# Two FFN weight sums change places in the upward pairs by seven products

## The reference, cut to what matters

```
def conv_ffn(h, w_up, conv_w, w_down):
    gu = causal_dwconv(h @ w_up, conv_w)        # h: 512 x 1024, w_up: 1024 x 5632
    g, u = jnp.split(gu, 2, axis=-1)
    return (jax.nn.silu(g) * u) @ w_down        # w_down: 2816 x 1024
...
x = x + conv_ffn(rmsnorm(x, norm_ffn_gain[i]), ffn_w_up[i], ffn_conv_w[i], ffn_w_down[i])
```

## Time and profile before

| | |
|---|---|
| time, median of 3 runs | 1220.42 us (1220.27 to 1220.99) |
| the profiled execution: time | 1220.91 us |
| the profiled execution: span | 1219.1 us |
| mean granted PE clock | 0.999 of full |
| PE busy | 1201.6 us (99%) |
| DVE, ACT, POOL busy | 757.1, 630.4, 740.3 us |
| first product of the first upward pair, end of the last | 856.37 us, 966.13 us |

### The profile page before, as it was taken

The page is one execution under the profiler, slowest core; times in us unless marked ns, Lnnn a source line. Parts: engine busy times, 40 slices in busy tenths (PEclk is TensorE's granted clock), DMA queues, the critical chain, the costliest instruction groups (busy, mean ns, idle before and its releaser), DMA issues.

```text
span 1219.1 us, 18895 instructions
## 1 busy us (share of the span) xinstructions
PE 1201.6 (99%) x6847; PEld 993.6 (82%) x6847; DVE 757.1 (62%) x1305; ACT 630.4 (52%) x1220; POOL 740.3 (61%) x561
## 2 busy tenths in 40 slices
PE   8999999999999999999999999999999999999997
PEld 6987777777888899987887777878888888889886
DVE  6555426757646777745697555447888865966234
ACT  6365535676644344455644666546545454333544
POOL 8674232353269776855384566548878775886842
PEclk9999999999999999999999999999999999999999
DMA  7322222122223333354142223323323343333332
GB/s 238 104 89 84 66 61 61 52 69 71 70 64 102 95 98 94 106 180 117 52 115 60 56 65 93 98 69 95 96 78 109 92 122 86 96 96 117 109 87 70
DMA packets 62437, 112.27 MB, mean 92 GB/s; under 512 B 6856, under 2 KB 11464, under 8 KB 62344
## 3 DMA queue, kind: packets, MB, share of 16 engines
q1 hardware_dynamic: 62200, 111.06, 31.6%
q10 hardware_dynamic: 144, 0.00, 0.0%
HBM read 108.87 MB, written 2.16 MB: 91 GB/s over the span
## 4 chain that ended last, share of the span: by engine, by line
PE 89%; DVE 6%; ACT 1%; issue 1%; POOL 1%; DMA 0%; SPq 0%; DVEq 0%; ACTq 0%; POOLq 0%
PE pb L1143 21%; PE pb L1144 20%; PE pb L1146 20%; PE pb L1205 4%; PE pb L1207 4%; PE pb L1206 4%; PE pb L1361 2%; DVE cv L2059 2%; PE pb L1337 2%; PE pb L1214 2%; PE pb L1304 1%; PE pb L1275 1%; PE pb L1277 1%; PE pb L1276 1%; PE pb L1258 1%
## 5 line engine op out<-in xcount | busy, mean ns | idle before, releaser
L2793 POOL TENSOR_TENSOR wlo<-raw,whi 128x512 fp32r<-128x512 f32 (+3 forms) x379 | 522.5, 1397 | 323.1 <-ACT whi L1554 322.1
L1143 PE MATMUL pb<-HH,whi 128*128 128x512 f32 x776 | 313.9, 405 | 0.0
L1144 PE MATMUL pb<-HL,whi 128*128 128x512 f32 x776 | 306.8, 395 | 0.0
L1146 PE MATMUL pb<-HH,wlo 128*128 128x512 f32 x776 | 306.1, 394 | 0.0
L1554 ACT ACTIVATE whi<-raw 128x512 fp32r<-128x512 f32 (+3 forms) x379 | 224.4, 614 | 107.7 <-PE pb L1146 55.5
L1143 PEld LDWEIGHTS pb<-HH,whi 128*128 128x128 f32 x776 | 146.2, 188 | 38.2 <-issue 4.6
L1144 PEld LDWEIGHTS pb<-HL,whi 128*128 128x128 f32 x776 | 146.0, 188 | 34.4 <-issue 2.9
L1146 PEld LDWEIGHTS pb<-HH,wlo 128*128 128x128 f32 x776 | 145.9, 188 | 34.5 <-POOL wlo L2793 0.4
L1690 ACT ACTIVATE P<-P,stat 128x256 f32<-128x256 f32 (+3 forms) x96 | 50.5, 527 | 78.5 <-DVE stat L2352 56.0
L2059 DVE SCALAR_TENSOR_TENSOR cv<-pb,vecs,cv 128x511 f32<-128x511 f32 x88 | 65.5, 745 | 4.8 <-ACT cv L1954 3.2
L2047 DVE TENSOR_TENSOR pb<-pb,rff 128x512 f32<-128x512 f32 x44 | 30.1, 694 | 38.5 <-PE pb L1146 31.7
(11 more groups left out here) (480 smaller groups left out, 2791.4 us busy)
## 6 DMA issues: line engine op xcount, KB each, us to landing
raw<-in_wall SPq DMA_DIRECT2D x368, 256.0 KB, 2.7
raw<-in_wall SPq DMA_DIRECT2D x8, 260.0 KB, 2.9
X<-in_xT SPq DMA_DIRECT2D x8, 256.0 KB, 5.6
X<-in_xT SPq DMA_DIRECT2D x2, 1024.0 KB, 7.3
outT<-PP SPq DMA_DIRECT2D x8, 256.0 KB, 2.5
raw<-in_wall SPq DMA_DIRECT2D x10, 192.0 KB, 2.4
raw<-in_wall SPq DMA_DIRECT2D x9, 128.0 KB, 2.3
cst<-in_cst SPq DMA_DIRECT2D x1, 832.0 KB, 7.8
```

Source lines behind the costliest of these rows:

```text
L1143: pe.do.matmul(b, hi, xh[k], start=start, stop=False, skip_group_check=tile[0] == "down")
L1144: pe.do.matmul(b, hi, xl[k], start=False, stop=False, skip_group_check=tile[0] == "down")
L1146: m = pe.do.matmul(b, lo, xh[k], start=False, stop=stop, skip_group_check=tile[0] == "down")
L2793: g.do.tensor_tensor(lo, x, hi.bitcast(F32), ALU.subtract).then_inc(*up(name, point))
```

## The change

In the upward pairs alone the unit and product order becomes A11, A22, S1, S2, S3, A12, S4: unit u+2 is now S1's, u+3 S2's. All of S1, S2 and S3 are summed by DVE, one behind the other, in split u+2. Nothing is computed otherwise. In `pair`, the steps that hang on product S2 keep their place behind it; as S1 is now no exception to the `split_to` ahead of a product, split u+7 is put before product S1, and u+8 and u+9 behind product S2.

```diff
+def factors(p):
+    return ("A11", "A22", "S1", "S2", "S3", "A12", "S4") if NGATE <= p < NUP else FACTORS
...
-                    for y in FACTORS:
+                    for y in factors(p):
                         self.unit_of[p, y] = len(self.units)
...
-        for x in FACTORS:
+        for x in factors(p):
             if not (NGATE <= p < NUP and x == "S2"):
                 self.split_to(self.unit_of[p, x] + LOOK)
             self.add("product7", p, x)
...
-                if x == "S2":
+                if x == ("S1" if kind(p) == "up" else "S2"):
                     for y in ("A22", "A21"):
                         v.wait_ge(*at("raw", plan.load_of[p, y]))
...
                     weights("S2", sums["S1"], arrived["A11"], ALU.subtract)
-                elif x == "S3":
+                if x == ("S1" if kind(p) == "up" else "S3"):
                     if p:
                         v.wait_ge(*at("wlo", plan.unit_of[p - 1, "S3"]))
                     weights("S3", arrived["A11"], arrived["A21"], ALU.subtract)
-                elif x == "A12" and kind(p) != "up":
+                if x == "A12" and kind(p) != "up":
```

## The result

The changed kernel takes 1225.91 us (median of 6 runs, 1224.12 to 1229.60), the kernel before 1220.41 us (6 runs, 1219.95 to 1220.99). The ratio is 1.0048, with an interval of 1.0037 to 1.0059: slower by more than the 0.2% that can be told from no change. The runs of the changed kernel lie 5.5 us apart, those of before 1.0 us; that spread is itself a finding. The profiled execution is the fastest of the six: 1224.12 us, span 1222.3 us, mean granted clock 0.997.

The account below looks back on a forecast made before the run. The prediction took DVE's loop, from S1's sum through u2 to the next S1 sum, to bound the upward pairs. 1.43 + 2.56 + 0.66 + 0.56 = 5.2 us gave 1226.1 us profiled, 1225.6 median; range 1224.1 to 1227.1.

Parts of the forecast that it names:

- DVE's round: Upward pairs: loop from S1's sum through u2 to the next S1 sum sets a pair's time, 22.79 us.
- S3's sum held up, then scaling, tap, high half, low half, PE: Pair 13: S3's sum ends at s+4.84 (s: start of S1's sum), putting u2 at s+10.32, 1.28 us later.
- POOL goes first at s+1.30: Pair 13, 1.30 us behind S1's sum's start: POOL's low half of A22 precedes S2's sum, which takes 1.82 us.
- DVE first: Rival at the port: S3's sum isn't held up, ends near s+3.66; +1.7 us, 1222.1; chance 0.17.
- the prediction's own signs for pair 13: S3's sum about 1.8 us, u2 near s+10.3, rounds 24 us; wrong if 0.7 us or rounds stay 22.8.
- Pair 6 delays u2 a little, but pair 9 ends that: Pair 6's delay adds nothing; in pair 9 u2 follows PE's S2, one product later: +1.43 us for DVE.
- -0.5 to +0.5 us a round: Earlier split of the next pair of units on ACT and POOL, beside DVE's steps: taken as 0, within these bounds.
- tile 16: Low half for its fourth weight unit hangs on pair 15's u2 and reaches PE late: +0.56 us.
- Rounds 11 and 13: Pairs 11 and 13: each round longer by u2's lateness, 2 x 1.28 = 2.56 us.
- Pair 15's end: End of pair 15 behind its S1 sum: s+14.25 instead of s+13.59, 0.66 us worse.
- made good: Rival: the loop's waits and earlier units swallow pair 9's 1.43 us and half the rest; +0.5 us, 1220.9; chance 0.10.
- The u2-to-S1 stretch is unchanged: DVE's work from u2 to the next pair's S1 sum keeps its length, 13.26 and 13.75 us before.

Follow-up runs that it names:

- e_both: Changed kernel with S3's sum behind the gate half's scaling, and the other half's scaling and two taps ahead of u2: 1216.32 us, ratio 0.9965.
- e_before_taps_ahead: Kernel before the change, with only a scaling and two taps of the tile ahead moved ahead of u2: 1219.77 us, ratio 0.9993.
- e_again: Changed kernel run once more, nothing edited, for a second profile and more times: 1227.00 us, ratio 1.0052.
- e_scaled_first: Changed kernel with S3's sum moved by one DVE instruction, behind the scaling of the gate half: 1221.25 us, ratio 1.0007.
- e_swap_only: Changed kernel's new order of products and units, but S3's sum at its old place behind the taps: 1223.78 us, ratio 1.0024.
- e_dve_first: Changed kernel, but POOL's low half of A22 waits for S1's sum in upward pairs, so DVE goes first: 1223.75 us, ratio 1.0025.
- e_sums_only: Old order of products and units, with S3's sum behind S1's and S2's as in the changed kernel: 1221.77 us, ratio 1.0009.
- e_pool_first: Changed kernel, but S2's sum waits for S1's high half in upward pairs, so POOL goes first: 1226.98 us, ratio 1.0052.

## Why the prediction was right, and where it was not

The forecast was 1225.6 us, the median 1225.9. It had two mechanisms, and the runs bear out both; it also had two things wrong that happen to offset each other in the median.

**The bound: right for the changed kernel.** No edit removed work, and new places for a few steps of DVE's round (with one tap of ACT) moved the time from 1225.9 to 1216.3 us (e_both). That the kernel before was bound by the same round is likely, but not shown: e_both beats it by 4.3 us without a wait of PE in the pairs, yet has the new order of products too, and the one test on the kernel before itself, e_before_taps_ahead, could not be told from no change.

**S3's sum held up, then scaling, tap, high half, low half, PE: right in e_again, step by step.** S3's sum 1.8 us (1.79), scaling at s+4.76 (937.95 - 933.18 = s+4.77), S2's product at s+8.28 (941.43, s+8.25), u2 at s+10.32 (10.31 to 10.36), the end at s+14.25 (14.22 to 14.28), rounds of about 24 us (24.06). PE waits once before S2, 2.0 us. e_scaled_first shows that S3's place ahead of the scaling is the cause.

**That POOL goes first at s+1.30: not a fact but a draw.** This is the step that failed. The prediction read 0.01 us between POOL and DVE as an order, and kept "DVE first" as a rival with 0.17. It is decided anew in each pair: first profile POOL, DVE, DVE; e_again POOL three times; e_swap_only POOL, POOL, DVE. The rival's numbers were as good as the forecast's: u2 at s+9.14 against 9.21 to 9.24 in e_dve_first, the end at s+13.07 against 13.10 to 13.17. A run is a mixture of both. By the prediction's own signs for pair 13, e_again shows the forecast and the first profile the rival (u2 at s+9.26, a round of 22.96).

**"Pair 6 delays u2 a little, but pair 9 ends that": wrong.** The term was 0 and measured 0.85 us in e_again; pair 9 came out at 1.58 for 1.43 (u2 itself 1.43 later: 12.28 behind S1's sum, 10.85 before). The cover looked for was PE's, in pair 9. The lateness reached PE before that, in tile 7: u2's own 0.32 us, and the longer tap steps beside three low halves. The latter is the edit costed at "-0.5 to +0.5 us a round"; the tap steps grew by 0.77. The place is the one that the prediction priced in tile 16 alone, the fourth weight unit behind a pair. The reading is from timelines; no run moves that third low half alone. e_sums_only, which lacks it, has no loss in pair 6 (31.45).

**Sizes.** With POOL first throughout, the sum 5.2 us measured 6.0 in the span (e_again) and 6.3 (e_pool_first); DVE first throughout, +1.7 measured 2.3 in the span and 3.0 in the median. Rounds 11 and 13: 2.56 forecast, 2.34 measured in e_again. Pair 15's end: 0.66 and 0.67. Tile 16: 0.56 and 0.45. So all but pair 6's term was sized right. That the median met the forecast to 0.3 us is luck: pair 6's loss and a share of DVE-first pairs go opposite ways, and the execution profiled (1224.12 us) is the fastest of the six, so what an execution near the median did is not shown. One sum of the rivals is wrong: "made good" swallows 1.43 us and half of the rest, which leaves 5.2 - 1.43 - 1.9 = 1.9 us (1222.3), not 0.5. Two of the chances are off by 0.02: by its own terms "within" adds up to 0.29 and "faster" to 0.05.

**The u2-to-S1 stretch is unchanged: right within its bounds** (13.74 and 13.70 against 13.93 and 13.75).

**Not foreseen: the fall of PE's clock** behind the longer wait, which added about 1.3 us to the pair's end in the two cases profiled, and to the round only in the one where it met S2's product.

**Open.** Why the clock fell behind two of the waits of about 2 us and not behind others; and whether falls account for the rest of the spread with POOL first (1225.9 to 1229.1 in e_pool_first). They would be large enough, but each kernel has one profiled execution.

## What to carry to other kernels

Where several in-order engines wait for each other in a ring, write down the ring's length per turn first: an instruction moved within it costs what it pushes back on the way to the next link, not its own length, and the slack of the bottleneck engine is no cover. Work that nothing waits for belongs where the ring waits (S3's sum behind the scaling, the taps ahead of u2). Here two such moves added up: 4.7 and 4.1 us alone and 9.6 us together, against the changed kernel's 1225.9. In the kernel before, where the wait was short, the second one alone gave nothing that can be told. Where two engines reach a shared port within hundredths of a microsecond, forecast both orders and force one, since the difference is decided in each execution.

## What the runs showed of the hardware

- A low half on POOL (1.30 us alone) and a sum of two SBUF operands on DVE (0.69 alone), issued within 0.02 us of each other, go in either order, and the order changes between pairs of one execution. Where POOL is first, S2's sum takes 1.81 to 1.84 us; where DVE is first, that takes 0.69 and POOL's low half 1.84 to 1.85 (first profile).
- With both engines at it back to back they take turns: behind S2's sum came POOL's waiting low half, and S3's sum took 1.77 to 1.79 us in every pair of e_again from 9 on. With DVE first in e_dve_first it took as long (1.78, 1.79): POOL's waiting low half then came between S2's sum and S3's.
- PE's granted clock stood at 0.50 (1.2 of 2.4 GHz) throughout stretches of 3.1 us that begin 1.4 and 0.6 us behind waits of 2.02 us (first profile, pair 11) and 2.03 us (e_pool_first, pair 11); it stayed at 1.00 behind waits of 2.06 us (e_pool_first, pair 13) and, in e_again, behind those of 2.03 and 2.01 us.
